# The gated-linear-attention layer rewritten as one block, with tile passes, direct context states and a four-unit scan

## The chip, the cores and the metric

One Trainium2 chip, one core of it. The metric is the device time of one launch in microseconds (us). The kernel runs on five engines that have their own instruction queues and meet only at semaphores: TensorE (PE, matrix products; PEld are its weight loads), VectorE (DVE), ScalarE (ACT), GpSimd (POOL), and SyncE (SP), which here issues DMA transfers.

## What is computed

Two blocks follow each other. The first block has two layers on 256 latent and 256 context positions of width 1024; the second block is not touched. Layer 0 mixes with a gated MLP, layer 1 with bidirectional gated linear attention (GLA); behind each mixer stands a residual with a layer norm, then PEER (top-k product-key experts), then again residual and norm. The part that matters is the mixer of layer 1:

```python
def gla_chunked(q, k, v, g, s0):            # chunks of 64 positions, 4 heads, dk=128, dv=256
    b = jnp.cumsum(g.reshape(bsz, n, GLA_CHUNK, h, dk), axis=2)
    b_end = b[:, :, -1:]
    q_in = q * jnp.exp(b); k_in = k * jnp.exp(-b); k_end = k * jnp.exp(b_end - b)
    att = jnp.where(mask, jnp.einsum('bnihd,bnjhd->bnhij', q_in, k_in), 0.0)
    o_intra = jnp.einsum('bnhij,bnjhe->bnihe', att, v)
    def step(state, inp):
        qc, kc, vc, dc = inp
        o = jnp.einsum('bihd,bhde->bihe', qc, state)
        state = dc[..., None] * state + jnp.einsum('bjhd,bjhe->bhde', kc, vc)
        return state, o
    ...

def gla_mixer(...):                         # last layer: need_ctx_out is False
    o_cf, s_f = gla_chunked(qc, kc, vc, gc[:, :, 0], s0)
    o_cb, s_b = gla_reverse(qc, kc, vc, gc[:, :, 1], s0)
    o_lf, _ = gla_chunked(ql, kl, vl, gll[:, :, 0], s_f)
    o_lb, _ = gla_reverse(ql, kl, vl, gll[:, :, 1], s_b)
    return gla_readout(o_lf + o_lb, rl, gn_g, w_out)
```

The projection `h @ w_in` gives q, k (512 columns each), v and the output gate r (1024 each) and 32 columns from which the decay logs g come (`log_sigmoid` of a second small product, over 16). In this last layer the outputs of the context positions are not needed, only the two states with which their scans end. Everything is float32.

## The kernel before

Positions stand on the 128 partitions in four tiles: tiles 0 and 1 are latent, 2 and 3 context. A large product `x @ w` is done at float32 precision from two 32-bit parts each, high and low (`split_matmul`): three matmuls for each block of 128 rows of w. The weights arrive in chunks of 256 rows by 512 columns (512 KB) in `landing`; ACT casts a chunk to its high part, DVE subtracts to get the low part, PE uses both.

The program before is a row of **stages** (`stage(k)`, line 84): a block in which each engine has its list, then a barrier of all engines and a clear of semaphores. Nothing of a later stage starts before the barrier. For layer 1 `first_layer` (line 2600) runs these, one behind the other: `residual_norm` of layer 0 on four tiles (line 486), `modulated` (459), then in `gla_mixer` (1581): `turn` (324: transposes and splits the activations), `gla_gates` (1399: the two small gate products, with `log_sigmoid`, 1437), `project` of 3072 columns for all four tiles (277, over `projection`, 184: eight landing slots, four split slots, per chunk all tiles before the next), two memsets, eight calls of `gla_tile` (1462: two directions by four tiles, two stages each), `head_norm` (420), `gate_rows` (1614), `turn`, `project` with w_out; then `residual_norm`, `modulated`, and in `peer` (1134): `turn`, `project_channels` (298), a stage for the scores, and `mix_experts` (1187). Each `gla_tile` first makes the cumulative decay logs with a matmul, exponentiates, weighs q and k; then in the second stage transposes, forms the scores `att`, and moves the state through its two chunks of 64. For context tiles only the state is moved.

In layer 0 the mixer was already written otherwise: `first_mix` (line 650) is one block in which each engine has one list written out by hand, with one semaphore for every kind of event and no barrier inside. Its functions `high`, `low_part`, `turn_job` and `take` have the same names and work as in the change.

The order everywhere is the order in which the code stands. No scheduler moves anything.

## Time and profile before

| | us |
|---|---|
| device time, median of 3 runs | 4376.91 (4375.4 to 4380.63) |
| device time of the profiled execution | 4377.48 |
| its span in the trace | 4375.7 |
| PE / DVE / ACT busy, share of the span | 80% / 62% / 30% |

The profile gives for each engine its busy time, and for each group of instructions (line, operation, operands) how long one takes and what it waited for. "PEclk" or "granted clock" is the clock of TensorE, as a share of its full 2.4 GHz: 0.5 is 1.2 GHz. The duration of one matmul is modelled and overlaps the next, so what a row of matmuls costs is read from the distance between their starts. A float32 matmul that is not split appears as two records. The rows are below, in the order in which the prediction comes to them.

### The profile page before, as it was taken

To read this page: it belongs to the slowest core of one execution; us is meant where nothing else is said; L and a number is where in the kernel's file an instruction comes from. 1 tells how busy PE (TensorE), PEld (TensorE's weight loads), DVE (VectorE), ACT (ScalarE), POOL (GpSimd) and SP (SyncE) were. 2 spreads that over 40 slices of the span, in tenths; PEclk is the share of its full clock that TensorE was granted. 3 is DMA by queue.
4 is the path that set the end of the run, shared out by engine and by line. 5 is a ranking of instruction groups with operands and counts; after the bars stand their busy time and mean duration, and the time that the engine had idled before them with its cause. 6 is when DMAs were issued, how large, how long until landed. Compare 5 with 4: busy or idle time off the path is not lost. (4 is left out here: it accounts for less than half of the span.)

```text
span 4375.7 us, 38555 instructions
## 1 busy us (share of the span) xinstructions
PE 3506.1 (80%) x13528; PEld 2238.9 (51%) x13528; DVE 2702.1 (62%) x5335; ACT 1331.8 (30%) x2307; POOL 735.9 (17%) x792
## 2 busy tenths in 40 slices
PE   8697777787777777496653777776899999999998
PEld 2386233333333332174443333332888797888896
DVE  7555766776776674432346677674766565766565
ACT  6432222222222221121011222221455454555453
POOL 0000433333333332000001333331000000000000
PEclk9898899999989998696676999998999999999999
DMA  9630999999999997030013999997655555565563
GB/s 355 222 110 33 420 422 421 421 422 421 421 421 421 421 421 288 26 115 2 1 44 137 421 422 421 421 421 290 203 169 172 184 174 173 161 178 167 173 185 126
DMA packets 282609, 1140.98 MB, mean 261 GB/s; under 512 B 26377, under 2 KB 28425, under 8 KB 184109
## 3 DMA queue, kind: packets, MB, share of 16 engines
q0 software_dynamic: 110592, 805.36, 44.3%
q1 hardware_dynamic: 170924, 331.58, 23.8%
q8 instruction: 106, 1.74, 0.2%
q10 hardware_dynamic: 900, 1.61, 0.1%
q14 instruction: 87, 0.70, 0.0%
HBM read 1137.30 MB, written 1.15 MB: 260 GB/s over the span
## 5 line engine op out<-in xcount | busy, mean ns | idle before, releaser
L133 PE MATMUL psum<-rows,diag 128*128 128x512 f32 x3072 | 1499.1, 645 | 483.2 <-ACT diag L1376 483.2
L133 PEld LDWEIGHTS psum<-rows,diag 128*128 128x128 f32 x3072 | 616.2, 206 | 1365.3 <-issue 733.2
L1339 DVE CUSTOM_DVE_ANT_0 rows<-rows,psum 128x1024 f32<-128x1024 f32 x768 | 937.5, 1221 | 586.3 <-DMA rows<-in_p_uv,place 585.8
L1227 POOL DMA_INDIRECT rows<-in_p_uv,place x768 | 723.5, 942 | 1184.3 <-PE psum L133 1138.8
L2589 DVE TENSOR_TENSOR weights_low<-landing,weights_high 128x1024 fp32r<-128x1024 f32 x400 | 488.1, 1223 | 393.5 <-ACT weights_high L2210 392.6
L2210 ACT CAST weights_high<-landing 128x1024 fp32r<-128x1024 f32 x400 | 417.7, 1047 | 571.5 <-PE psum L133 389.0
L133 PE MATMUL psum<-weights_high,hT_high 128*128 128x512 f32 x960 | 380.7, 397 | 30.5 <-DVE weights_low L264 29.2
L1376 ACT ACTIVATE diag<-ident,weight 128x128 f32<-128x128 f32 x768 | 245.3, 390 | 471.9 <-DVE weight L1315 471.9
L133 PE MATMUL psum<-weights_high,hT_low 128*128 128x512 f32 x960 | 375.5, 391 | 0.0
L133 PE MATMUL psum<-weights_low,hT_high 128*128 128x512 f32 x960 | 375.3, 391 | 0.0
L1367 ACT ACTIVATE acted<-dots 128x4 f32<-128x4 f32 x192 | 39.4, 205 | 1038.4 <-DVE dots L1339 1038.4
L1815 PE MATMUL psum<-hT_high,weights_high 128*128 128x256 f32 x1024 | 291.7, 285 | 3.4 <-DVE weights_low L2589 3.4
L1816 PE MATMUL psum<-hT_low,weights_high 128*128 128x256 f32 x1024 | 290.9, 284 | 0.0
L1817 PE MATMUL psum<-hT_high,weights_low 128*128 128x256 f32 x1024 | 290.8, 284 | 0.0
L133 PEld LDWEIGHTS psum<-weights_high,hT_high 128*128 128x128 f32 x960 | 181.4, 189 | 70.5 <-issue 32.6
L133 PEld LDWEIGHTS psum<-weights_high,hT_low 128*128 128x128 f32 x960 | 181.1, 189 | 38.6
L133 PEld LDWEIGHTS psum<-weights_low,hT_high 128*128 128x128 f32 x960 | 181.5, 189 | 36.9 <-issue 0.5
L1815 PEld LDWEIGHTS psum<-hT_high,weights_high 128*128 128x128 f32 x1024 | 197.7, 193 | 5.0 <-issue 4.9
L1816 PEld LDWEIGHTS psum<-hT_low,weights_high 128*128 128x128 f32 x1024 | 197.8, 193 | 0.1
L1817 PEld LDWEIGHTS psum<-hT_high,weights_low 128*128 128x128 f32 x1024 | 197.7, 193 | 0.0
L640 DVE TENSOR_TENSOR weights_low<-landing,weights_high 128x1024 fp32r<-128x1024 f32 x96 | 114.9, 1217 | 6.5 <-ACT weights_high L607 2.9
L607 ACT CAST weights_high<-landing 128x1024 fp32r<-128x1024 f32 x96 | 100.8, 1050 | 30.9 <-DMA landing<-in_w_mod 30.0
(363 smaller groups left out, 4165.3 us busy)
## 6 DMA issues: line engine op xcount, KB each, us to landing
landing<-in_w_in SPq DMA_DIRECT2D x192, 512.0 KB, 3.9
landing<-in_w_ff SPq DMA_DIRECT2D x128, 512.0 KB, 4.4
landing<-in_w_mod SPq DMA_DIRECT2D x96, 512.0 KB, 8.4
landing<-in_w_br SPq DMA_DIRECT2D x32, 512.0 KB, 4.0
rows<-in_p_uv,place POOLq DMA_INDIRECT x768, 26.5
landing<-in_b_w_in SPq DMA_DIRECT2D x24, 512.0 KB, 4.6
landing<-in_a_w_in SPq DMA_DIRECT2D x16, 512.0 KB, 4.8
landing<-in_p_w_q SPq DMA_DIRECT2D x16, 512.0 KB, 4.9
```

The lines of the kernel that those rows point to most:

```text
L133: return k.nc.tensor.matmul(out, lhsT, rhs, start=first, stop=last)
L607: nc.scalar.copy(weights.high[:, n % splits], landing[:, n % ring]).then_inc(chunk_high, 1)
L640: nc.vector.tensor_tensor(weights.low[:, n % splits], landing[:, n % ring], weights.high[:, n % splits].bitcast(F32), ALU.subtract).then_i ...
L1227: k.nc.gpsimd.indirect_dma_start(rows[:, n % ROW_RING, :], None, k.given["p_uv"], bass.IndirectOffsetOnAxis(place[:, g % 4, c:c + 1], 0))\
L1339: V.tensor_tensor_reduce(u, u, token, 1.0, 0.0, ALU.mult, ALU.add, dots[:, g % 4, c:c + 1]).then_inc(k.dots_done, 1)
L1367: k.nc.scalar.activation(acted[:, g % 4, 4 * q:4 * q + 4], dots[:, g % 4, 4 * q:4 * q + 4], ACT.Gelu_apprx_tanh).then_inc(k.gelu_done, 1)
L1376: k.nc.scalar.activation(diag[:, n % DIAG_RING, :], k.ident[:, :], ACT.Copy, scale=weight[:, g % 4, c:c + 1]).then_inc(k.diag_set, 1)
L1815: nc.tensor.matmul(to, mine.high, tokens.high, start=first, stop=False, skip_group_check=True)
L1816: nc.tensor.matmul(to, mine.high, tokens.low, start=False, stop=False, skip_group_check=True)
L1817: mm = nc.tensor.matmul(to, mine.low, tokens.high, start=False, stop=last, skip_group_check=True)
L2210: S.copy(weights.high[:, n % SPLITS], landing[:, n % LANDING]).then_inc(chunk_high, 1)
L2589: V.tensor_tensor(weights.low[:, n % SPLITS], landing[:, n % LANDING], weights.high[:, n % SPLITS].bitcast(F32), ALU.subtract).then_inc(ch ...
```

## The change

`first_layer` becomes `first_block`. Layer 0 keeps `first_mix` and `mix_experts`; behind them, everything from the residual norm of layer 0 to the scores of layer 1 becomes one new function, `second_mix`, one block without a barrier inside, and `mix_experts` follows as before. `residual_norm` is still used once, at the end. `gla_gates`, `gla_tile`, `gla_mixer`, `head_norm`, `modulated`, `turn`, `projection`, `peer` and others go. What `second_mix` does otherwise than the stages before:

- **Passes.** One pass is one tile (128 positions) by one group (512 columns, four chunks): 24 matmuls of 128x512. The four chunks of a group stay resident through its passes (`SPLITS = 5`, `LANDING = 3`); in the last pass of a group each chunk is set free as it is used. k and v are projected for four tiles, q and r only for the two latent ones.
- **Norms.** The residual norm of layer 0 and the modulation of layer 1 are folded: the gains and shifts are multiplied together once (`gains`), so that h comes from x in two operations; the normed x itself is made later. The same is done before PEER.
- **Gates.** One split product for both directions (`gates_low`), the bias as a 17th row of the second product, the factor 1/16 in the mask matrices, the `1 +` in the Ln's bias.
- **Context states** as direct sums (`context_sums`, `first_state`): exp of the sum of all later (or earlier) logs, times k, times v over both context tiles. No scan over the context.
- **Latent scan in four units** (`UNITS`): (direction, tile) = (0,0), (1,1), (0,1), (1,0). Between their parts stand passes 15, 16 and 17.
- **Readout.** The layer norm's 1/root goes in as a diagonal matrix in place of the identity in the transposes of y, the gain `b_gn_g` into w_out's split.

The core of the diff, with what the prediction speaks of:

```diff
+def second_mix(k, x, h, g, scores):
+    LANDING, SPLITS = 3, 5
+    GROUPS = [(w_in, NC), (w_in, 2 * NC), (w_in, 3 * NC), (w_in, 0), (w_in, 4 * NC), (w_in, 5 * NC),
+              (w_out, 0), (w_out, NC), (w_q, 0), (w_q, NC)]
+    ORDER = (2, 3, 0, 1)
+    PASSES = [(of, t) for of in range(3) for t in ORDER] + [(of, t) for of in range(3, 6) for t in (0, 1)] \
+        + [(of, t) for of in range(6, 8) for t in (1, 0)] + [(8, None), (9, None)]
+    UNITS = ((0, 0), (1, 1), (0, 1), (1, 0))
...
+        @block.sync
+            sp.dma_start(g2_rows[:, 1, :], row(0, 1, 5)).then_inc(g2_landed[1], 16)
+            for j, part in enumerate((1, 0)):
+                sp.dma_start(m_rows[:, j, 1, :], row(1, 1, part)).then_inc(m_rows_landed[1], 16)
+            for n in range(COUNT):
+                if n >= LANDING:
+                    sp.wait_ge(chunk_low, n + 1 - LANDING)
+                sp.dma_start(landing[:, n % LANDING, :, :], ...)
+                if n == 16:
+                    wait_pass(sp, 9)
...
+                if n == 18:
+                    sp.wait_ge(ctx_keys, 4)
...
+        @block.tensor
+            for j, (t, p) in enumerate(((2, None), (3, 0), (0, 1), (1, None))):
+                pe.wait_ge(h1_set, j + 1)
+                turn_tile(h, t)
+                if p is not None:
+                    pe.wait_ge(turn_low, 2 * p + 2)
+                    one_pass(p)
+            for p in (2, 3):
...
+                one_pass(p)
+            gates_low()
+            for p in range(4, 14):
+                if p == 6:
...
+                    gates_z(0)
+                if p == 8:
+                    gates_z(4)
+                if p == 11:
...
+                    context_sums()
+                if p == 12:
...
+                    decays()
+                if p == 13:
...
+                    first_state(0)
...
+                    unit_decays(0)
+                pe.wait_ge(act_taken, p - 1)
+                one_pass(p)
+            first_state(1)
+            one_pass(14)
+            for u in range(4):
...
+                    pe.wait_ge(o_set, u)
+                unit_turn(u)
+                unit_update(u, 0)
+                if u < 3:
+                    pe.wait_ge(unit_exp, u + 1)
+                    unit_decays(u + 1)
...
+                unit_att(u)
+                if u < 3:
+                    pe.wait_ge(act_taken, 15 + u)
+                    one_pass(15 + u)
+                if u < 2:
+                    unit_update(u, 1)
+                unit_out(u)
+            for t, p in ((1, 18), (0, 19)):
+                pe.wait_ge(y_set, p - 17)
+                pe.wait_ge(y_diag_set, p - 17)
+                turn_tile(y, t, y_diag)
...
+                one_pass(p)
+            for p in (20, 21):
+                pe.wait_ge(dve_taken, p - 19)
+                one_pass(p)
+            for j, t in enumerate((1, 0)):
+                pe.wait_ge(h2_set, j + 1)
+                turn_tile(h, t)
...
+            queries(8)
+            queries(9)
+            pe.wait_ge(keys_landed, 32)
+            score(0)
+            score(1)
...
-def first_layer(k, x, layer, h):
-    streams = 1 if layer == DEPTH - 1 else 2
-    if layer == 0:
...
-    else:
-        modulated(k, x, h, 2, layer, 1, 0)
-        gla_mixer(k, h)
-        residual_norm(k, x, h, streams, layer, 2, 0)
-        modulated(k, x, h, streams, layer, 4, 3)
-        peer(k, h, 2 * streams, layer)
-    residual_norm(k, x, h, streams, layer, 5, 1)
+def first_block(k, x, h):
...
+        second_mix(k, x, h, g, scores)
+        mix_experts(k, h, scores, 2, 1)
+    residual_norm(k, x, h, 1, 1, 5, 1)
```

What stood in a row before and what stands there now, at three places. First DVE, at the start of the stretch, right behind the last of layer 0's experts. Before (`rows`, `affine` are the broadcast gate and gain rows):

```order
L504 TENSOR_TENSOR h<-h,rows 128x1024 [waits loaded0]
L504 TENSOR_TENSOR h<-h,rows 128x1024 x3
L507 SCALAR_TENSOR_TENSOR x<-x,h 128x1024 [waits vector_step]
L507 SCALAR_TENSOR_TENSOR x<-x,h 128x1024 x3
L387 BN_STATS stats<-x 128x6 [waits vector_step]
L387 BN_STATS stats<-x 128x6 x7
L390 BN_AGGR moments<-stats 128x2 [waits vector_step]
L390 BN_AGGR moments<-stats 128x2 x3
```

Now (`g_rows` the gate rows, `m_rows` the modulation, `n_rows` the norm's gain and shift):

```order
L1545 TENSOR_TENSOR h<-h,g_rows 128x1024 [waits g2_landed1]
L1547 SCALAR_TENSOR_TENSOR x<-x,h 128x1024 [waits gla_step]
L1550 BN_STATS stats<-x 128x6 [waits gla_step]
L1550 BN_STATS stats<-x 128x6
L1552 BN_AGGR moments<-stats 128x2 [waits gla_step]
L1554 TENSOR_SCALAR spread<-moments 128x1 [waits gla_step]
L1558 SCALAR_TENSOR_TENSOR r<-m_rows,n_rows 128x1024 [waits gla_n_rows_landed,gla_m_rows_landed1]
L1559 SCALAR_TENSOR_TENSOR m_rows<-m_rows,n_rows 128x1024
L1561 TENSOR_TENSOR m_rows<-m_rows,r 128x1024 [waits gla_step]
L1575 SCALAR_TENSOR_TENSOR h<-x,moments,m_rows 128x1024 [waits gla_step]
L1579 RECIPROCAL inverse<-root 128x1 [waits gla_root]
L1581 SCALAR_TENSOR_TENSOR h<-h,inverse,m_rows 128x1024 [waits gla_step]
```

Before, DVE does one step for all four tiles and then the next; now it carries one tile through all steps, and the second, third and fourth tile follow in the same manner. Second, PE in the scan of a latent tile. Before (`z` holds v, `ke` the weighed k):

```order
L133 MATMUL psum<-qT,kT 128x128 [waits vector_step]
L133 MATMUL psum<-qT,kT 128x128 x7
L133 MATMUL psum<-z,ke 128x256 x4
L133 MATMUL psum<-z,att 128x256 [waits vector_step]
...
L133 MATMUL psum<-z,ke 128x256 [waits states]
L133 MATMUL psum<-z,ke 128x256 x3
L133 MATMUL psum<-state,qT 128x256 x4
L85 UNCONDITIONAL_BRANCH
L1473 UNCONDITIONAL_BRANCH [waits barrier_Pool_Activation_PE_DVE_SP_release]
```

Now, unit 0 (`h` holds v, `unit_e` the weighed q and k, `masks` the cumulative matrices):

```order
L1069 MATMUL psum<-ident,unit_e 128x128 [waits unit_keys,unit_clear,state_set]
L1069 MATMUL psum<-ident,unit_e 128x128 x7
L122 MATMUL psum<-h,unit_e 128x256 x4
L122 MATMUL psum<-g,masks 128x512 [waits unit_exp]
L122 MATMUL psum<-g,masks 128x512
L122 MATMUL psum<-qT,kT 128x64 [waits k_copied,q_copied,gla_act_taken]
L122 MATMUL psum<-qT,kT 128x64 x7
L122 MATMUL psum<-weights_high,latT_high 128x512 [waits gla_low,gla_act_taken]
...
L122 MATMUL psum<-h,unit_e 128x256 [waits stepped]
L122 MATMUL psum<-h,unit_e 128x256 x3
L122 MATMUL psum<-h,att 128x256 [waits stepped,att_set]
L122 MATMUL psum<-state,qT 128x256 x2
```

The barrier behind the tile is gone, the next unit's decay sums and a whole pass of the projection stand between the scores and the outputs, and the states of both chunks are taken in one accumulation. Third, DVE at the end, between the last pass of w_out and the queries of PEER (new rows only; before, this was `residual_norm`, `modulated` and `turn` in stages of their own):

```order
L1715 TENSOR_TENSOR h<-psum,kk 128x512 [waits gla_step,gla_used]
L1718 SCALAR_TENSOR_TENSOR x<-x,h 128x512 [waits gla_dve_taken]
L1720 BN_STATS x_stats<-x 128x6 [waits gla_step]
L1725 BN_AGGR x_moments<-x_stats 128x2 [waits gla_step]
L1727 TENSOR_SCALAR x_spread<-x_moments 128x1 [waits gla_step]
L1728 SCALAR_TENSOR_TENSOR h<-x,x_moments,late 128x1024
L1731 RECIPROCAL x_inverse<-x_root 128x1 [waits gla_root]
L1733 SCALAR_TENSOR_TENSOR h<-h,x_inverse,late 128x1024 [waits gla_step]
L1530 TENSOR_TENSOR weights_low<-landing,weights_high 128x1024 [waits gla_high]
L1536 TENSOR_TENSOR latT_low<-psum,latT_high 128x4x128 [waits gla_turn_high] x4
```

What was three stages is one chain of eight operations and the four splits of the turned tiles, and a chunk's low part stands inside it.

## Rows read from the trace of the kernel before

**Rows 1.** Start and end of the stretch, timeline: start us, us, engine, line, what.

```profile
1735.58 1.01 ACT L1357 COPY h<-psum 128x1024 f32<-128x1024 f32 x1 [7.16 <-PE psum L133]
1742.42 4.63 DVE L504 TENSOR_TENSOR h<-h,rows 128x1024 f32<-128x1024 f32 x4 [15.31 <-DMA rows<-modulation]
2375.41 0.48 DVE L1236 MAX8 s<-scores 128x8 f32<-128x128 f32 x2
```

**Rows 2.** Stages of the stretch: busy PE, PEld, DVE, ACT, POOL; granted clock, DMA share, GB/s.

```profile
1735.00:1768.00 33.00, 0.54 (x2) 0.00 (x0) 24.62 (x30) 2.50 (x3) 0.00 (x0) 0.54 0.18 64
...
1794.00:1840.00 46.00, 39.36 (x80) 10.00 (x80) 6.89 (x10) 0.00 (x0) 0.00 (x0) 0.85 0.06 16
1840.00:1862.00 22.00, 0.00 (x0) 0.00 (x0) 13.44 (x4) 9.80 (x4) 0.00 (x0) 0.50 0.00 0
1862.00:2006.00 144.00, 133.50 (x576) 109.99 (x576) 43.38 (x48) 25.26 (x24) 0.00 (x0) 0.96 0.27 88
2006.00:2248.00 242.00, 138.31 (x448) 98.02 (x448) 76.98 (x154) 18.62 (x41) 11.34 (x16) 0.66 0.00 1
2248.00:2300.00 52.00, 28.13 (x112) 23.06 (x112) 26.04 (x47) 15.20 (x17) 0.00 (x0) 0.75 0.27 92
2300.00:2325.00 25.00, 0.00 (x0) 0.00 (x0) 17.22 (x20) 0.20 (x1) 0.00 (x0) 0.52 0.31 103
2325.00:2375.00 50.00, 37.88 (x240) 35.58 (x240) 18.61 (x29) 13.39 (x20) 0.31 (x1) 0.80 0.24 86
```

**Rows 3.** Start of the projection on DVE and PE, and PE near its end, timeline.

```profile
1867.08 1.23 DVE L264 TENSOR_TENSOR weights_low<-landing,weights_high 128x1024 fp32r<-128x1024 f32 x1 [5.65 <-ACT weights_high L228]
1868.46 0.77 PE L133 MATMUL psum<-weights_high,hT_high 128*128 128x512 f32 x1 [29.23 <-DVE weights_low L264]
...
1869.45 0.63 PE L133 MATMUL psum<-weights_high,hT_low 128*128 128x512 f32 x1
1869.87 0.63 PE L133 MATMUL psum<-weights_high,hT_high 128*128 128x512 f32 x1
...
1998.39 0.39 PE L133 MATMUL psum<-weights_high,hT_high 128*128 128x512 f32 x1
1998.62 0.39 PE L133 MATMUL psum<-weights_low,hT_high 128*128 128x512 f32 x1
```

**Rows 4.** Unsplit float32 products on PE in `gla_gates`, the scan and `turn`, timeline.

```profile
1785.28 5.40 PE L340 MATMUL psum<-ident,h 128*128 128x128 f32 x32 [49.74 <-PEq L88]
...
1807.62 1.02 PE L133 MATMUL psum<-hT_high,wg 128*16 128x512 f32 x2
1808.48 1.02 PE L133 MATMUL psum<-hT_low,wg 128*16 128x512 f32 x2
...
2027.25 3.77 PE L133 MATMUL psum<-z,ke 64*128 64x256 f32 x8
...
2091.20 1.99 PE L133 MATMUL psum<-state,qT 128*128 128x256 f32 x8
```

**Rows 5.** Groups of DVE and ACT in the stretch: busy us, mean ns, idle before.

```profile
L264 DVE TENSOR_TENSOR weights_low<-landing,weights_high 128x1024 fp32r<-128x1024 f32 x32 | 38.3, 1221 | 46.3 <-ACT weights_high L228 46.1
L228 ACT CAST weights_high<-landing 128x1024 fp32r<-128x1024 f32 x32 | 33.3, 1051 | 112.1 <-PE psum L133 98.3 <-DMA landing<-in_b_w_in 12.3 <-PEq L234 1.6
L1578 DVE TENSOR_TENSOR o<-o,psum 128x512 f32<-128x512 f32 x16 | 11.0, 685 | 0.4
```

**Rows 6.** DMA issues in two parts of the stretch: KB each, median us to landing.

```profile
rows<-modulation SPq DMA_DIRECT2D x6, 512.0 KB, 5.4
landing<-in_b_w_out SPq DMA_DIRECT2D x8, 512.0 KB, 9.3
```

**Rows 7.** `first_mix` of layer 0, windows: its passes, and its queries.

```profile
310.00:320.00 10.00, 10.00 (x46) 8.28 (x45) 7.34 (x10) 1.61 (x2) 0.00 (x0) 1.00 0.00 0
360.00:370.00 10.00, 9.71 (x83) 9.47 (x81) 1.36 (x3) 1.77 (x4) 0.00 (x0) 1.00 0.01 2
```

**Rows 8.** A table load on ACT in the scan, timeline.

```profile
2019.16 1.28 ACT L1498 ACT_TABLE_LOAD   x1
```

1187 lines of the change are left out of this document (731 added, 456 removed).

## The prediction

> **What bounds the kernel now.** I first took the two ends of the stretch that the change replaces. The last expert product of layer 0 ends as ACT starts its copy at 1735.6; the experts of layer 1 begin with DVE's first MAX8 at 2375.4 [rows 1]. The stretch is 639.8 us long. Outside it the instructions are the same, so 4377.5 - 639.8 = 3737.7 us stay, measured against the profiled execution, which lies 0.6 us above the median of the three runs. The only question is how long the new stretch is.
>
> The table of stages [rows 2] shows why it can shrink. PE is busy for about 380 of those 640 us, at whatever clock it was granted. In the scan (242 us) it is busy 138 us at a granted clock of 0.66; in the norms (33 and 25 us) and in the log-sigmoid (22 us) it does nothing and DVE works alone. Only the projection (144 us, busy 133.5, clock 0.96) is filled. So no engine bounds the stretch; barriers do, each with one chain of dependent work behind it.
>
> **Prices.** At full clock split 128x512 matmuls start 0.227 us apart, and just after idle 0.43 (1869.45 to 1869.87, 1998.39 to 1998.62) [rows 3]. A pass of 24 is thus 5.44 us. An unsplit float32 product of 512 columns (two records) costs 0.86 (1807.62 to 1808.48), four of 256 columns about 1.75 to 2.0 at full clock and 3.8 at half, and a 128-column transpose 0.17 on a mean of slow and fast, 5.40 us for 32 [rows 4]; I take 0.21 cold and 0.12 warm. DVE needs 1.22 for 128x1024 and 0.69 for 128x512, ACT 1.05 for a chunk [rows 5]. A 256-column split matmul is 0.12 (83 in 9.7 us) [rows 7].
>
> **The new stretch, step by step.** I walked the four lists (PE, DVE, ACT, SP) against each other with these prices.
>
> Head, until the second pass is issued. The first row load still lands 6.8 us after the start (1735.6 to 1742.4) [rows 1]. Then DVE alone sets the pace, because PE's first pass needs low parts that stand behind norms in DVE's list. Up to `low_part(3)` that list holds three residual sums with their moments (2 x 1.22 + 2 x 0.61 + 0.4 for the small steps = 4.05 each), two gain folds (3.66 each), three norms (2.65 each), four turn jobs (0.69) and four low parts (1.22): 12.2 + 7.3 + 8.0 + 2.8 + 4.9 = 35.2 us. To this come waits. Eleven transfers of 512 KB are now asked for at once on two queues, where the old stage asked for four; at the 5.4 us that a row takes to land behind its neighbours [rows 6], the norm rows come about 1.5 us and the chunks that ACT's first root stands behind about 3 us after DVE wants them: 4.6. The last quarter of pass 0 at half clock (2.6) and the turn of tile 0 (1.7) follow: 4.3. Head = 6.8 + 35.2 + 4.6 + 4.3 = 50.9. Those waits could be nothing (-4.6), or each load could take as long as the slowest chunk landing, 9.3 us [rows 6] (+5); I stay near the 5.4, since these are the same kind of load.
>
> Middle, on PE, from pass 1 to pass 14. Here PE is the longest engine. Thirteen of the fourteen passes 1 to 14 at 5.44 each = 70.7, pass 1 itself 5.44 + 2.4 for twelve cold matmuls (12 x 0.2) = 7.8; a turn 1.2; `gates_low` 48 matmuls of at most 256 columns at 0.12 = 5.7 (it replaces 32 unsplit products at 0.86, 27.5 us); the eight gate products 6.9; six context sums 5.2; `decays` 3.8 (16 products of two columns, bounded by their weight loads at 0.24); two `first_state` 6.9; the first unit's sums 1.7. Sum 109.9. DVE has about 45 us of work in this time and ACT about 55, six table loads among it, so both hide. What they could cost is a wait at `gates_z` or `context_sums`: there the logs must be ready two passes later, and by my walk they are ready 2 and 6 us early. Of the q and r projections of context tiles six passes are gone, 32.6 us at full clock.
>
> Units, u = 0 to 3. Each has the transposes (1.0), an update (1.7), the next unit's sums (1.7), scores (1.7), a pass (5.4), a second update (1.7), outputs, 12 products of 256 columns (5.2), and ACT's or DVE's two copies before the next unit may overwrite the banks (1.4): 19.8, twice. Unit 2 has no second update, but DVE's copies for ACT's: 18.3. Unit 3 has neither pass nor sums to cover its copies and masks (2.6): 13.8. Sum 71.7. The eight old scan tiles took 242 [rows 2].
>
> Tail, to the first MAX8. Turn and split of y tile 1 (3.2), pass 18 (5.4), wait for the second readout and its diagonals (1.0), turn and split of tile 0 (3.0), passes 19 to 21 (16.3); then almost nothing on PE while DVE does three low parts (3.7), takes the last result (2.1), ends the norm of tile 0 (2.9), does one more low part (1.2) and four splits (2.8): 12.7; queries, 8 chunks of 24 x 0.12, and 2.4 cold = 25.4; scores and the last copy 7.7; barrier 1.3. Sum 76.0.
>
> Together 50.9 + 109.9 + 71.7 + 76.0 = 308.5. Not in it are about 35 hand-overs between engines at 0.15 us, as between a low part's end (1867.08 + 1.23) and PE's start (1868.46) [rows 3], and two more cold starts of 2.4 in the tail: I add 10. The bounds of this term are 0 and, if each hand-over cost 0.7 us as one small DVE operation does [rows 5], 25. The new stretch is 319 us, and **the forecast is 3737.7 + 319 = 4057 us**.
>
> **A rule weighed.** A table load on ACT takes 1.28 us here [rows 8], and the new list has eight in the stretch (sqrt, exp and ln twice, exp, silu, sqrt). I count them at that price, beside PE's passes. The Trainium skill ("ScalarE: Activation LUTs", What ACT_TABLE_LOAD costs) says that a switch also pays a drain, together about 2.66 us. By that page, and if all eight were on the path, the estimate would be 4068; the trace shows only the 1.28.
>
> **Rivals.**
>
> A, the clock stays low in the units. In the scan before, PE had a granted clock of 0.66 though it was busy more than half of the time [rows 2], and the first matmuls after a wait go at half speed [rows 3]. Unsplit products then cost double (3.8 against 2.0) [rows 4]. Against it: in the units the waits are 1 to 2 us and dense passes stand between, and `first_mix`, written in the same way, has 1.00 throughout its passes [rows 7]. About 64 us of the units are PE work; at 0.66 they cost 33 more, at half 64: 4090, at the far end 4121. The Trainium skill ("TensorE: Matmul & The Clock Gate", HAM oscillation) describes this for kernels whose bursts are shorter than their waits; by that rule units without passes would stay cold, and here only unit 3 is one.
>
> B, a list waits in the wrong order. Each engine's list is fixed, and one late event (ACT's logs before `context_sums`, a chunk of w_out behind `late` in SP's queue, DVE's chain before the queries) holds all behind it. Nothing in the profile before shows such a list for this layer; PE's idle rests in `first_mix`'s passes are nil [rows 7]. If the waits sum to 30 us instead of 10 the time is 4077, if to 45, 4092.
>
> C, fewer waits than I allow: the 10 us don't appear and the head's 4.6 neither: 4043.
>
> D, slower than before. The ring is shorter: three landing slots instead of eight, and every chunk's transfer is asked for only when the low part of three chunks earlier is done. If the transfers did not overlap at all, a chunk would cost landing 9.3 + cast 1.05 + low part 1.22 = 11.6 us, 40 chunks 463, and with the head's 51 and a tail of 30 the time would be 4282. It becomes slower than before only if a chunk costs over 14 us; at 16 it would be 3737.7 + 640 + 81 = 4459. Nothing in the rows comes near.
>
> E, the change doesn't do what it says: PE's list shows passes between the parts of the units, so only the waits are open.
>
> **Chances.** Forecast 55% (its own range 4045 to 4073), A 12%, B 19%, C 12%, D 1%, something else 1%. The range from 4032 to 4098 takes in C, B and A's nearer end and the bounds of head and hand-overs. Faster by over 0.2% (8.8 us, about what a measurement of this kernel can tell from no change) 98%, within it 1%, slower 1%.
>
> **What will show it.** In the changed profile: DVE's first sum about 6.8 us after the experts' last product, pass 1 on PE about 51 us after it; granted clock 1.0 and starts 0.227 apart from pass 2 on; pass 14 ending near 161 us; units about 20, 20, 18 and 14 us long; an idle PE of about 10 us before the queries and the first MAX8 about 319 us after the start. Wrong would be: a clock below 0.9 in the units (A), a wait of over 3 us in front of a pass (B), or `mix_experts` and what follows changed by more than 5 us, which would break the first subtraction.

## The result and the profile after

The changed kernel takes **4050.61 us** (median of four runs, 4047.85 to 4052.42), the kernel before 4376.15 (four runs beside it, 4375.07 to 4380.63): a ratio of 0.925, 95% interval 0.9239 to 0.9262, so 325.5 us less. The forecast was 4057, with a range from 4032 to 4098. The profiled execution took 4050.69 us, its span is 4048.9, and the mean granted clock over it is 0.936.

The ends of the stretch in the changed kernel, in the timeline (start us, us, engine, line, operation); they answer to [rows 1]:

```profile
1736.40 1.01 ACT L2001 COPY h<-psum 128x1024 f32<-128x1024 f32 x1 [7.16 <-PE psum L122]
...
1742.87 1.23 DVE L1545 TENSOR_TENSOR h<-h,g_rows 128x1024 f32<-128x1024 f32 x1 [14.95 <-DMA g_rows<-modulation]
...
2050.76 0.48 DVE L1880 MAX8 s<-scores 128x8 f32<-128x128 f32 x2
```

The stretch is 2050.76 - 1736.40 = 314.4 us long instead of 639.8. Outside it are 4050.69 - 314.4 = 3736.3 us, against 3737.7 before: the experts did not change, and all of the gain lies in the stretch.

What stood there before as stages [rows 2] is now one block. The windows over it (length, then busy time and count of PE, PEld, DVE, ACT, POOL; granted clock, DMA share, GB/s): the whole stretch, then head, middle, units and tail as the prediction cut them, then the four units.

```profile
1736.40:2050.76 314.36, 250.47 (x1228) 204.33 (x1228) 169.32 (x253) 114.84 (x178) 3.23 (x6) 0.90 0.29 91
1736.40:1792.40 56.00, 13.70 (x49) 10.87 (x49) 38.07 (x47) 10.56 (x15) 1.24 (x3) 0.61 0.47 153
1792.40:1900.80 108.40, 106.70 (x490) 84.52 (x489) 45.49 (x52) 53.58 (x79) 1.85 (x2) 0.98 0.34 108
1900.80:1975.30 74.50, 68.41 (x325) 53.82 (x324) 41.81 (x87) 27.57 (x47) 0.00 (x0) 0.98 0.19 57
1975.30:2050.80 75.50, 61.66 (x368) 55.13 (x368) 43.99 (x68) 23.18 (x38) 0.14 (x1) 0.91 0.18 56
1900.80:1921.40 20.60, 19.46 (x93) 15.08 (x91) 11.14 (x20) 8.87 (x14) 0.00 (x0) 1.00 0.34 103
1921.40:1942.10 20.70, 19.51 (x93) 15.16 (x93) 10.23 (x20) 3.88 (x8) 0.00 (x0) 1.00 0.00 1
1942.10:1960.80 18.70, 17.36 (x84) 13.78 (x84) 12.40 (x24) 8.12 (x14) 0.00 (x0) 1.00 0.29 86
1960.80:1975.30 14.50, 12.08 (x56) 9.80 (x57) 8.04 (x25) 6.70 (x11) 0.00 (x0) 0.88 0.09 35
```

The same query over the old stretch, as one window of the kernel before:

```profile
1735.58:2375.41 639.83, 382.58 (x1488) 281.83 (x1488) 241.68 (x358) 89.55 (x119) 11.79 (x18) 0.74 0.14 46
```

Put side by side, the two whole-stretch rows split the gain in two. PE's busy time fell from 382.6 to 250.5 (132 us: less work, and the same work at 0.90 of the clock instead of 0.74). Its idle time fell from 257 to 64 us (193 us). DVE's busy time fell too, from 242 to 169, while ACT's rose from 90 to 115: ACT took over work, beside PE.

| part | forecast | measured |
|---|---|---|
| outside the stretch | 3737.7 | 3736.3 |
| head, to pass 1 | 50.9 | 56.0 |
| middle, pass 1 to unit 0 | 109.9 | 108.4 |
| units | 71.7 (19.8, 19.8, 18.3, 13.8) | 74.5 (20.6, 20.7, 18.7, 14.5) |
| tail | 76.0 | 75.5 |
| hand-overs, not placed | 10 | none is left over |

So three things were to be explained: the head is 5.1 us too long, the units 2.8, and the 10 us for hand-overs did not appear. The head first. ACT in its first 26 us (ACTq is its DMA queue):

```profile
1741.32 0.60 ACTq L1279 DMA_DIRECT2D wg<-in_b_w_in  x1
1741.95 7.72 ACTq L1282 DMA_DIRECT2D w<-in_b_w_gate  x1
...
1750.49 3.83 ACTq L1282 DMA_DIRECT2D w<-in_b_w_gate  x1
...
1758.46 0.45 ACTq L1289 DMA_DIRECT2D gain<-in_b_gn_cols  x1
1758.96 1.99 ACT L1309 CAST weights_high<-landing 128x1024 fp32r<-128x1024 f32 x2 [21.55 <-issue]
1760.96 1.28 ACT L1320 ACT_TABLE_LOAD   x1
1762.26 0.20 ACT L1320 ACTIVATE root<-spread 128x1 f32<-128x1 f32 x1
```

And DVE, which needs that root:

```profile
1749.67 1.23 DVE L1558 SCALAR_TENSOR_TENSOR r<-m_rows,n_rows 128x1024 f32<-128x1024 f32 x1 [2.57 <-DMA n_rows<-in_ln_b]
...
1762.49 0.16 DVE L1579 RECIPROCAL inverse<-root 128x1 f32<-128x1 f32 x1 [7.88 <-ACT root L1320]
```

DVE had the variance ready at 1747.1 and waited for the root from 1754.6 on; the root, 0.2 us of work, came at 1762.3. Ahead of it in ACT's list stood the issue of its loads (until 1758.9, with two issues that took 7.72 and 3.83 us), the casts of the first two chunks, and a table load. DVE's waits in the head are 2.57 + 7.88 = 10.45 us where the prediction had 4.6. In the DMA issues of this window a chunk of w_in took 14.8 us to land and the norm's rows 8.7 and 10.7, where [rows 6] had 9.3 for a chunk and 5.4 for a row:

```profile
landing<-in_b_w_in SPq DMA_DIRECT2D x3, 512.0 KB, 14.8
...
n_rows<-in_ln_g ACTq DMA_DIRECT2D x1, 512.0 KB, 8.7
n_rows<-in_ln_b ACTq DMA_DIRECT2D x1, 512.0 KB, 10.7
```

Two theories for the head stood against each other. **Issue**: ACT's sequencer is blocked by its own 20 loads. **Data and order**: eleven and more transfers of 512 KB share the DMA engines, and the root stands in the wrong place of ACT's list.

### The profile page after: what moved, and what is told of

The parts are those of the page before. It is cut to its first block and busy times, and to the rows that moved or that the text cites. A ratio compares the mean times of both kernels' runs of the same rounds, so it can differ in the third digit from the quotient of the medians.

```text
span 4048.9 us, 37069 instructions
## 1 busy us (share of the span) xinstructions
PE 3380.2 (83%) x13268; PEld 2162.0 (53%) x13268; DVE 2630.6 (65%) x5231; ACT 1357.4 (34%) x2366; POOL 729.1 (18%) x780
## 5 line engine op out<-in xcount | busy, mean ns | idle before, releaser
L122 PE MATMUL psum<-weights_high,hT_high 128*128 128x512 f32 x768 | 304.7, 397 | 1.3 <-DVE hT_low L2649 1.3
L122 PE MATMUL psum<-weights_high,hT_low 128*128 128x512 f32 x768 | 299.8, 390 | 0.0
L122 PE MATMUL psum<-weights_low,hT_high 128*128 128x512 f32 x768 | 299.8, 390 | 0.0
L122 PEld LDWEIGHTS psum<-weights_high,hT_high 128*128 128x128 f32 x768 | 144.7, 188 | 32.2 <-issue 1.8
L122 PEld LDWEIGHTS psum<-weights_high,hT_low 128*128 128x128 f32 x768 | 144.6, 188 | 30.9
L122 PEld LDWEIGHTS psum<-weights_low,hT_high 128*128 128x128 f32 x768 | 144.8, 189 | 29.1 <-issue 0.5
L315 ACT CAST weights_high<-landing 128x1024 fp32r<-128x1024 f32 x96 | 100.8, 1050 | 30.9 <-DMA landing<-in_w_mod 30.0
```

The lines of the kernel that those rows point to most:

```text
L122: return k.nc.tensor.matmul(out, lhsT, rhs, start=first, stop=last)
L315: nc.scalar.copy(weights.high[:, n % splits], landing[:, n % ring]).then_inc(chunk_high, 1)
```

## Experiments on the head

**Small loads away from ACT.** The gate weights, masks and small vectors (15 loads) are issued by POOL, which has little to do there.

```diff
+            # in POOL's list, behind its first three memsets
+            pool.wait_ge(wg_clear, 1)
+            for j in range(2):
+                pool.dma_start(wg[...], w_in[...]).then_inc(wg_landed, 16)
...
-            act.wait_ge(wg_clear, 1)
-            for j in range(2):
-                act.dma_start(wg[...], w_in[...]).then_inc(wg_landed, 16)
...
```

> The changed kernel with one edit: the 15 small loads of second_mix (gate weights, masks, member, gain) are issued by POOL instead of ACT. In the changed kernel ACT spends 1738.0 to 1758.9 issuing them, 7.7 and 3.8 us of it on the two loads that stand behind the gathers of the gate columns, and DVE waits 7.9 us for the first root. Theory 1 (ACT's list is the cause, the issue blocks behind the gathers): chunk 0 has landed long before, the root comes 6 to 9 us earlier, DVE's wait falls to under 2 us, head 56 to 48..50 us, time 4050.6 to 4042..4045. Theory 2 (the data are the cause: eleven big loads share the DMA engines, and chunk 0 lands late anyway): the wait stays over 5 us and the time within 3 us of 4050.6.

Measured: 4046.83 us (4043.14 to 4052.09), ratio to before 0.925 (0.9235 to 0.9266); stretch 310.0 against 314.4. DVE's reciprocal stood 24.2 us after the start instead of 26.1. ACT, in this run's timeline:

```profile
1754.62 1.05 ACT L1310 CAST weights_high<-landing 128x1024 fp32r<-128x1024 f32 x1 [19.08 <-DMA landing<-in_b_w_in]
1756.11 1.05 ACT L1310 CAST weights_high<-landing 128x1024 fp32r<-128x1024 f32 x1 [0.44 <-DMA landing<-in_b_w_in]
1757.17 1.28 ACT L1321 ACT_TABLE_LOAD   x1
1758.46 0.20 ACT L1321 ACTIVATE root<-spread 128x1 f32<-128x1 f32 x1
```

ACT's queue was now free and ACT still waited, for the chunk: "<-issue" has become "<-DMA landing". That alone would say that the issue cost almost nothing. But the chunk did not land when it did before. The first chunk's load in the changed kernel, and in this run:

```profile
landing<-in_b_w_in SPq DMA_DIRECT2D x1, 512.0 KB, 13.8
```

```profile
landing<-in_b_w_in SPq DMA_DIRECT2D x1, 512.0 KB, 16.7
```

In the changed kernel it was issued at 1739.3 and had landed at 1753.1, 16.7 us after the start, and ACT came to it at 1758.96: its own issues held it for 5.8 us. In this run it landed 20.1 us after the start, and DVE's wait for the rows grew from 2.57 to 4.34 us. The small loads were now all issued 11.5 us after the start instead of 22.5, beside the large ones; whether that, or the other queue, made the large ones land later was not taken apart. So both theories hold a part: the issue was removed (DVE's wait for the root fell from 7.88 to 4.29), later landings took most of it back, and the head gained 2 us. The result lies between the two expectations. Of the 4.4 us by which the stretch is shorter, 1.7 are a higher clock in unit 3 (below). The medians are only 3.8 us apart, about as much as the runs of one kernel scatter, so these sizes rest on the traces.

**The root first.** On top of that, the norm's two row loads stand first in ACT's queue, and the first root ahead of the casts.

```diff
-            act.dma_start(g2_rows[:, 0, :], row(0, 0, 5)).then_inc(g2_landed[0], 16)
             for j, name in enumerate(("ln_g", "ln_b")):
                 act.dma_start(n_rows[:, j, :], ...)
+            act.dma_start(g2_rows[:, 0, :], row(0, 0, 5)).then_inc(g2_landed[0], 16)
...
+            first_root(0)
             high(0)
             high(1)
-            first_root(0)
```

> small_on_pool with two more moves: the norm's second row load stands first on ACT's queue, and ACT's first root stands ahead of its casts of chunks 0 and 1 in ACT's list. Theory ACT's order: DVE's first reciprocal stood 24.2 us after the start in small_on_pool, of which 4.3 us were a wait for a root that was queued behind two casts and a table load; with the root ahead of them the reciprocal comes 3 to 5 us earlier and the stretch is 305 to 307 us long against 310.0, time 4042 to 4044. Rival, the landing itself: the rows and chunks share the DMA engines, and what DVE gains it waits again for the first low part, because chunk 0 lands no earlier and is now cast later: the reciprocal is earlier but pass 0 and pass 1 stay where they were, 35 us and about 54 us after the start, and the time stays 4047.

Measured: 4044.51 us (4040.97 to 4046.39), ratio 0.9237 (0.9221 to 0.9252); stretch 307.6. ACT:

```profile
1746.34 0.20 ACT L1321 ACTIVATE root<-spread 128x1 f32<-128x1 f32 x1 [4.60 <-DVE spread L1555]
1755.66 1.04 ACT L1310 CAST weights_high<-landing 128x1024 fp32r<-128x1024 f32 x1 [9.12 <-DMA landing<-in_b_w_in]
```

The root now comes at once, and DVE's reciprocal 19.7 us after the start, 4.5 earlier than in the run before, within what the theory of ACT's order expected (3 to 5). Of the 4.5, 4.3 are the wait for the root. Moving the norm's rows forward brought only 0.2: DVE still waits 4.11 us at the same place, now for the modulation rows (`m_rows`); pass 0 begins 30.8 us after the start instead of 35.3 and pass 1 49.6 instead of 54.1, so the rival (nothing moves on, because the chunk lands no earlier) is refuted. The chunk did land no earlier (20 us after the start in both), but DVE has other work until then. The stretch shortened by 2.3 only: at the first unit 3.6 us of the 4.5 were left, and unit 3 gave back 1.6 (its clock, below). The time and the stretch lie about 0.5 us above the ranges that were expected.

## Experiments on the tail

PE's longest wait after the units is for the second normed tile. In the changed kernel DVE stood as follows before it, and PE behind it:

```profile
2003.96 3.49 DVE L1530 TENSOR_TENSOR weights_low<-landing,weights_high 128x1024 fp32r<-128x1024 f32 x3
2007.37 0.68 DVE L1715 TENSOR_TENSOR h<-psum,kk 128x512 f32<-128x512 f32 x1
```

```profile
2012.58 1.12 PE L992 MATMUL psum<-ident,h 128*128 128x128 f32 x4 [7.39 <-DVE h L1733]
```

Three low parts that only the queries need stand before the result that everything waits for.

**Tail reordered.** They go behind the last norm, and the turn of the first tile ahead of it. ACT's list is put in the same order (its part of the edit is left out here).

```diff
             last_norm(0)
-            for n in range(33, 36):
-                low_part(n)
+            for j in range(12, 14):
+                turn_job(j, latT, 1 - (j - 12) // 2)
             take(21)
             last_norm(1)
-            low_part(36)
-            for j in range(12, 16):
+            for j in range(14, 16):
                 turn_job(j, latT, 1 - (j - 12) // 2)
-            for n in range(37, 40):
+            for n in range(33, 40):
                 low_part(n)
```

> The changed kernel with one edit: in the tail, DVE's low parts of chunks 33 to 35 and 36 move behind the last norm and the last turn jobs (ACT's cast of chunk 36 likewise), since PE can't use them before the queries start. They stand 3.5 + 1.2 us in DVE's chain from the end of pass 21 to the queries. Theory 1 (that chain is the path): PE's start of the queries moves 4 to 5 us earlier against pass 21's end, time 4050.6 to 4046 +- 1. Theory 2 (the queries then wait for their second chunk's low part, as they wait for the first now): gain under 2 us.

Measured: 4048.21 us (4045.51 to 4049.22), ratio 0.9247 (0.9232 to 0.9263); tail 73.1 instead of 75.4. Only half of what was expected. DVE's list shows why:

```profile
2003.75 1.29 DVE L1538 TENSOR_TENSOR latT_low<-psum,latT_high 128x512 fp32r<-128x512 f32 x2 [1.37 <-ACT latT_high L1314]
2004.96 0.68 DVE L1717 TENSOR_TENSOR h<-psum,kk 128x512 f32<-128x512 f32 x1
```

The turn jobs that took the low parts' place cost 1.29 and, being at the end of a chain over PE and ACT, a wait of 1.37 in front of them: of the 3.4 us of low parts only 0.8 were gained (PE's wait is 6.63 instead of 7.39), and the rest of the 2.3 came behind it. One late event at the head of a list again held what stood behind it.

**Both early moves** (small loads on POOL, the tail, and in the head low part 3 ahead of DVE's second gain fold and third norm):

> The changed kernel with the edits of small_on_pool and tail_order together, and low_part(3) in DVE's head before the second gain fold instead of behind the third norm, so that pass 0 does not wait for it. If the two waits are independent the gains add: -8, -4.5, and -2 from the head's order, time 4036 +- 3. If ACT's and DVE's lists only move the wait elsewhere, 4041 or more.

Measured: 4043.51 us (4039.05 to 4048.11), ratio 0.9242 (0.9227 to 0.9257), stretch 306.9. That is the second of the two expectations: the gains did not add up to 4036. The first unit begins 4.3 us earlier than in the changed kernel and the tail is 1.5 shorter; the other 1.7 are the clock of unit 3.

**All moves, and all turn jobs behind `last_norm(1)` on DVE** (against the run before; the two moves of the run with the root first are not shown again).

```diff
             last_norm(0)
-            for j in range(12, 14):
-                turn_job(j, latT, 1 - (j - 12) // 2)
             take(21)
             last_norm(1)
-            for j in range(14, 16):
+            for j in range(12, 16):
                 turn_job(j, latT, 1 - (j - 12) // 2)
             for n in range(33, 40):
                 low_part(n)
```

> root_first, and low_part(3) ahead of one of DVE's turn jobs, and in the tail the last norm and the turn of tile 0 ahead of low parts 33 to 39. Theory: PE's wait for the second turn of the tail (7.4 us in the changed kernel, of which 3.5 us were low parts ahead of it in DVE's list) goes, the low parts fall beside passes 18 to 21, and the tail is 4 to 5 us shorter than 75.4; together with the head the stretch is 301 to 304 us and the time 4036 to 4041. Rival: the low parts are then late for passes 19 to 21 and PE waits for them instead; the tail stays at 73 to 75 and the time is 4042 to 4045, as the run with both earlier moves.

Measured: **4038.44 us** (4037.17 to 4039.20), ratio to before 0.9226 (0.921 to 0.9241); stretch 303.3, tail 71.5. It is the fastest of all: its slowest run is 8.6 us below the fastest of the changed kernel. PE's wait for the second turn:

```profile
2002.05 1.97 PE L1006 MATMUL psum<-ident,h 128*128 128x128 f32 x8 [4.35 <-DVE h L1736]
```

From 7.39 to 4.35, as the theory expected, and the rival (PE waits for low parts instead) is refuted. So of the changed kernel's 314.4 us, 11 were the order of a few instructions: 6.9 before the first unit, 4.0 in the tail. Unit 3 has the lower clock in both kernels, so the clock has no part in this difference.

## Experiments on the units

**Passes ahead of the units.** The three passes that stand inside units 0 to 2 run before them, with their casts and copies on ACT and their low parts on DVE.

```diff
             one_pass(14)
+            for u in range(3):
+                pe.wait_ge(act_taken, 15 + u)
+                one_pass(15 + u)
             for u in range(4):
...
                 unit_att(u)
-                if u < 3:
-                    pe.wait_ge(act_taken, 15 + u)
-                    one_pass(15 + u)
```

> The changed kernel with one edit: passes 15, 16 and 17 stand in front of the four scan units instead of inside units 0 to 2 (casts, low parts and takes of their chunks moved with them). Theory 1 (the passes in the units cover the waits for copies, masks and state, some 2.5 us per unit, and nothing else): three units lose that cover, +7 to +9 us, granted clock stays at 1.0 in the units, 4058. Theory 2, rival A of the prediction (without dense passes PE's clock falls in the units as in the old scan, 0.66): units of about 20 us each instead of 15, +20 to +35 us, 4071 to 4086. Theory 3 (nothing to cover): within 3 us.

Measured: 4057.11 us (4053.84 to 4059.78), ratio 0.9272 (0.9256 to 0.9287); 6.5 us slower by the medians, 3.0 in the trace. The window of its four units:

```profile
1916.87:1975.79 58.92, 50.58 (x254) 39.44 (x252) 34.14 (x79) 17.40 (x34) 0.00 (x0) 1.00 0.11 36
```

The prediction's rival A was that the clock would be low in the units. Here they have no dense passes between their parts, PE is idle 14% of the time, and the clock is 1.00 throughout. What the passes covered is read from units 0 to 2, which ran at 1.00 in both kernels: they take 46.1 us here (1916.87 to 1962.99), and in the changed kernel 60.0, of which three passes are 16.3, so 43.7. The three passes covered 2.4 us inside the units. Another 2.4 stand ahead of the units, where the passes now follow each other and each waits for ACT to clear its banks, three times like this:

```profile
1898.48 0.49 PE L122 MATMUL psum<-weights_high,latT_high 128*128 128x512 f32 x1 [0.68 <-ACT r L1337]
```

So interleaving is worth 4.8 us in the trace, 1.6 a pass. The trace's stretch is only 3.0 us longer, because unit 3 ran at full clock here and gave 1.7 back. The medians say 6.5, and the profiled execution is the fastest of this run's four; what is left between 3.0 and 6.5 is open. The first theory (cover lost, clock kept) came out, a little below its 7 to 9 us.

The prediction took from the Trainium skill ("TensorE: Matmul & The Clock Gate", HAM oscillation) that units without passes would stay cold. The Trainium skill describes there bursts of work that are shorter than the waits between them. Here the waits are 1.0 to 1.4 us and the work between them is several times as long, so the units without passes are another case, and this run doesn't test it. The low clock of the old scan (0.66, [rows 2]) went with longer idle rests, such as the 5.05 us in a row of the next section; here PE's longest wait is 1.4.

Unit 3 alone is a small case of the rival. It has a granted clock of 0.88 and takes 14.5 us in the changed kernel; in the run with the small loads on POOL the same instructions ran at 1.00:

```profile
1956.04:1968.84 12.80, 10.39 (x56) 8.64 (x57) 8.04 (x25) 6.71 (x11) 0.00 (x0) 1.00 0.10 38
```

That is 1.7 us, in one unit. The kernels with both early moves, with the passes ahead and with doubled passes also have 12.8 us there; those with the root first, with the tail reordered and with all moves have 14.3 to 14.5. PE's wait in front of it is 1.38 us in all of them; which of their differences decides it stays open. With two landing slots (below) it is worse.

## Parts of the change alone, in the kernel before

**Direct context states only.** The four context tiles of the scan are replaced by one load of masks and one stage, everything else as before.

```diff
-            for direction, tiles in ((0, (2, 3, 0, 1)), (1, (3, 2, 1, 0))):
+            context_states(k, z, g, state)
+            for direction, tiles in ((0, (0, 1)), (1, (1, 0))):
...
+                matmul(k, k.psum[:, 0, :], after[:, :], g_of(0, 2), True, False)
+                matmul(k, k.psum[:, 0, :], every[:, :], g_of(0, 3), False, True)
...
+                            mm = matmul(k, k.psum[...], ce[:, 2 * d + t, a * P:(a + 1) * P],
+                                        z[:, 2 + t, D + a * DV:D + (a + 1) * DV], t == 0, t == 1)
```

> The kernel before with one part of the change alone: the context states as direct sums. Four of the eight scan tiles (about 24.2 us each) are gone; in their place stand one load of three 128x128 masks and one stage of six 256-column products, four exponentials, four multiplications, sixteen 256-column products and four copies, about 25 to 30 us with its load. Theory: the barriers and chains of the scan tiles are a large part of what the change gains, and this part alone brings 97 - 27 = 70 us: 4306, between 4300 and 4316. Rival: most of the gain is the overlap of passes with everything else, and the direct sums bring less because their unsplit products run at a low clock and the stage is one chain: the new stage costs 45 us or more, the time is 4325 or above.

Measured: 4298.89 us (4296.16 to 4304.10), ratio 0.9824 (0.9807 to 0.984): **77.6 us** less. PE in the new stage, up to the first remaining tile:

```profile
2016.54 2.05 PE L133 MATMUL psum<-g,after 128*128 128x512 f32 x2 [15.63 <-PEq L88]
...
2024.67 7.07 PE L133 MATMUL psum<-z,ce 128*128 128x256 f32 x32
2033.49 1.10 PE L133 MATMUL psum<-g,prefix 128*128 128x512 f32 x2 [1.75 <-PEq L88]
...
2075.84 0.45 PE L1516 MATMUL psum<-ident,qi 128*128 128x128 f32 x1 [5.05 <-PEq L88]
```

From its first product to that of the next tile the stage takes 17 us, and its load puts 3.5 us in front (15.63 of idle time where the kernel before has 12.13); together they stand for four tiles of about 24. The estimate of 27 for both was high, and the time lies 1 us below the expected range (4300 to 4316), on the side of the theory. The last row is PE's first product of a latent tile's second stage, behind an idle rest of 5.05 us, in which the chain through ACT and DVE runs.

**Split gate product only.**

```diff
+        split(k, wg[:, :, :], wgs.part(slice(None), slice(None), slice(None)))
...
-                        for part in (hT.high, hT.low):
-                            mm = matmul(k, k.psum[0:GLA_RANK, j, :], wg[...], part[:, b, :].bitcast(F32), ...)
+                        mm = split_matmul(k, k.psum[0:GLA_RANK, j, :], wgs.part(...), hT.part(slice(None), b), ...)
```

> The kernel before with one part of the change alone: the low-rank gate product as split products. 32 unsplit products of 0.86 us (27.5 us) become 48 split ones at 0.227 (10.9 us), and a split of the 128x512 gate weights is added (about 2 to 3 us, with its barrier). Theory, price of unsplit products: 14 us faster, 4362. Rival, the clock: the products stand in a stage that begins cold, so both forms run partly at half clock, and 48 cold ones of 0.43 cost 20.6: 4 us faster only, 4372.

Measured: 4362.77 us (4360.01 to 4365.18), ratio 0.9968 (0.9957 to 0.998): **13.7 us** less. The first product of this run, and the one behind the last:

```profile
1800.92 0.58 PE L133 MATMUL psum<-hT_high,wgs_high 128*16 128x512 f32 x1 [9.91 <-PEq L88]
...
1815.30 1.12 PE L133 MATMUL psum<-w,low 16*128 16x512 f32 x2 [0.77 <-DVE low L1428]
```

The 48 products took 13.6 us rather than 10.9, since the first go at 0.43 (1801.31, 1801.73, 1802.16), but the old ones start cold too and took 29.3 (1799.09 to 1828.38): the difference came out as computed.

**Ten empty stages** ahead of the scan:

```diff
+            for _ in range(10):
+                with stage(k):
+                    pass
             for direction, tiles in ((0, (2, 3, 0, 1)), (1, (3, 2, 1, 0))):
```

> The kernel before with ten stages that hold no work, put between the log-sigmoid and the eight scan tiles. It prices one barrier. Theory, barriers are cheap by themselves and cost by the chains they end: 1.1 to 1.5 us each, as the barrier behind the stretch's last copy, so 11 to 15 us, time 4388 to 4391. Rival, each barrier costs more (instruction lists of five engines, a first wait): 2.5 us or more each, 25 us in all, 4402; then the stages of the old stretch would have cost a large part of the 326 us that the change gained.

Measured: 4383.57 us (4382.05 to 4387.35), ratio 1.0011 (1.0002 to 1.0021), which is 1 to 9 us for ten. PE's first product of the scan in the kernel before, and in this run:

```profile
2014.08 2.05 PE L133 MATMUL psum<-g,prefix 128*128 128x512 f32 x2 [12.13 <-PEq L88]
```

```profile
2024.64 2.05 PE L133 MATMUL psum<-g,prefix 128*128 128x512 f32 x2 [19.56 <-PEq L88]
```

PE is idle 7.43 us longer: **0.74 us for a barrier** whose stage is empty, below both expectations. (The whole stretch is 10.6 us longer in this trace; 3.9 of that stand before PE's rest, where the two kernels are the same, and show how much one trace differs from another.) The barriers themselves were a small part of what was gained. What they cost in the old stretch is what stood idle on both sides of them, such as the 5.05 us above.

## Is the middle bound by PE, and is three landing slots enough?

**Six passes run twice** (4, 5, 6, 8, 9, 10, over the same operands, so nothing else changes):

```diff
-                for pair in range(4):
+                for pair in range(4) if p not in (4, 5, 6, 8, 9, 10) else (0, 1, 2, 3, 0, 1, 2, 3):
```

> The changed kernel with passes 4, 5, 6, 8, 9 and 10 computed twice over the same operands (the same sums are started again, so the output is unchanged): the PE work of six passes more, 144 products, as many as the change leaves out for the context's queries and readout gates. Theory, PE sets the middle and those six passes were worth their full 32.6 us: middle 141, time 4083. Rival, the middle is in part set by what DVE and ACT prepare (high and low parts every 2.3 us of DVE's time, 45 us in all): then the extra products fill waits and the time rises by less than 27 us, under 4078.

Measured: 4080.78 us (4078.48 to 4085.27), ratio 0.9322 (0.9305 to 0.9339): **30.2 us** more by the medians. The window from pass 1 to the first unit:

```profile
1791.30:1930.60 139.30, 139.30 (x635) 111.89 (x634) 45.68 (x52) 54.44 (x79) 1.85 (x2) 0.98 0.26 84
```

139.3 against 108.4 in the changed kernel: 30.9 of the 32.6 us that 144 products at 0.227 cost. The rest filled a wait of 1.7 us for ACT that PE has there. So PE bounds the middle, and the six passes that the change leaves out were worth 30 us (31 in the middle; unit 3 gave 1.7 back at full clock).

**Two landing slots instead of three.**

```diff
-    LANDING, SPLITS = 3, 5
+    LANDING, SPLITS = 2, 5
```

> The changed kernel with two landing slots instead of three for the 40 chunks of weights; it is the point from which the rival of a too short ring decides. Theory, slack: a chunk takes some 6 to 9 us to land behind its request and PE uses two per 5.4 us, so with two slots a pass of two chunks can't be faster than about one landing and one cast and low part (9 to 11 us): the middle's 14 passes grow from 5.4 to 8 or more and the time rises by 30 to 60 us: 4080 to 4110. Rival, the transfers are short when few are queued (512 KB at the 370 GB/s measured in the head is 1.4 us): time rises by under 8 us.

Measured: 4065.40 us (4064.07 to 4067.82), ratio 0.9286 (0.9269 to 0.9303): 14.8 us more, below the one expectation and above the other. The stretch grew by 16.9: 3.7 before the units, 6.3 in them, 6.9 in the tail. Of the 6.3 most is one unit's clock. PE now waits 3.34 us in front of unit 3 (1.38 in the changed kernel), and the unit itself takes 18.8 us for 14.5:

```profile
1965.08:1983.90 18.82, 16.41 (x56) 13.17 (x57) 8.04 (x25) 6.70 (x11) 0.00 (x0) 0.64 0.08 27
```

The other 2.0 are that longer wait. So rival A is real in kind: 2 us more of waiting, and unit 3 ran at 0.64 with the same instructions. Whether the longer wait alone did it was not tested. ACT's wait for the chunks of the queries' weights in the tail (what, total, times, longest), in the changed kernel and in this run:

```profile
ACT weights_high L1309 <- DMA landing<-in_p_w_q: 2.3, 1, 2.3
```

```profile
ACT weights_high L1309 <- DMA landing<-in_p_w_q: 6.0, 2, 5.2
```

PE's wait for the second normed tile grew with it, since DVE's low parts and norms stand in one list:

```profile
PE psum L992 <- DVE h L1733: 12.1, 2, 11.0
```

My expectation took every pass to use new chunks. In the passes up to the units it doesn't hold: a group of four chunks serves four passes, later two, so the next group has 22 or 11 us to land, and two slots do almost as well as three. In the units and the tail a late chunk delays a list in which ACT and DVE have other duties, and PE waits for these. With three slots ACT's one wait of this kind in the tail is 2.3 us.

## Why the prediction came out 6 us high

The parts that were summed give 308.5, 5.9 less than the 314.4 measured; with the 10 for hand-overs the forecast was 4.1 more. Outside the stretch the time is 1.4 less than was taken over. So two errors of opposite sign (head and units too short, a term for waits that did not come) stood behind a result that is 6 us off, and a part of that nearness is luck.

**Where it was right.** The cut of the time into what stays and a stretch (3737.7 against 3736.3) and the statement that barriers and their chains bound the old stretch: 193 of the 325 us are PE's idle time. The middle (109.9 against 108.4) was summed from product counts and the distances of [rows 3, 4 and 7], and the doubled passes show that this was the right kind of sum, since PE is busy in 106.7 of those 108.4 us. Two small terms in it offset each other: pass 1 was priced with 2.4 us of cold products and ran at full clock from its third product on, and a wait of 1.7 us for ACT was not in the sum. The gate product was priced by [rows 4] at 27.5 against 5.7 for its new form; alone in the old kernel a split form saved 13.7 where the same prices gave 14. The tail came out at 75.5 for 76.0, with its idle rest before the queries at 11.7 us (2005.19, where PE runs dry, to 2016.84, where the queries start, with the second tile's turn in it) for 12.7. The table loads are 1.28 us here too, eight in the block, and the next activation starts 1.29 or 1.30 after each load's start:

```profile
1829.74 1.28 ACT L1349 ACT_TABLE_LOAD   x1
1831.03 2.19 ACT L1349 ACTIVATE x<-x 128x512 f32<-128x512 f32 x4
1833.24 1.28 ACT L1353 ACT_TABLE_LOAD   x1
```

The drain that the Trainium skill adds ("ScalarE: Activation LUTs", What ACT_TABLE_LOAD costs) can't be seen in these rows, and the estimate of 4068 worked out from that page's figure was further off than the sum from rows.

**Step that was mis-sized: the head's waits (4.6, measured 10.45).** "The norm rows come about 1.5 us and the chunks that ACT's first root stands behind about 3 us after DVE wants them." The mechanism is there, with both of its releasers in the trace (2.57 for the rows, 7.88 for the root). The price of 5.4 us for a landing, taken from a stage with four transfers at once, was wrong for a dozen: the rows took 8.7 and 10.7, a chunk 14.8. The upper bound that the text gave (5 us more, by the 9.3 of the slowest chunk landing) happened to be nearly what was measured, but for another reason. The first chunk had landed at 1753.1, before DVE asked for the root. What held the root until 1762.3 was the issue of 20 loads on ACT's queue, until 1758.9, and behind it two casts and a table load (1.99 + 1.28). The prediction counts the eleven large transfers and not what their and the 15 small loads' issue costs ACT; it had seen that the root stands behind the chunks and had not asked what the casts and the table load add there. The run with the small loads on POOL shows that removing the issue alone brings 2 us, since the large loads then land later; the root's place in ACT's list was worth 4.3 us more. The rest of the head was right: 56.0 - 6.5 - 10.45 = 39.1 for the list and the start of PE, summed as 35.2 + 4.3 = 39.5.

**Step that was wrong: the 10 us of hand-overs.** The prediction added 35 hand-overs at 0.15 and two cold starts, beside sums that had been made from distances between starts and from walks that already ended in waits. Measured against the parts, nothing is left for them: middle -1.5, tail -0.5, and what the head and the units took beyond their sums has other causes. A hand-over counts only where PE waits, and in the middle it does once. In the units, where waits do end parts, they were priced (1.4, measured 1.16 twice):

```profile
1921.42 1.09 PE L1069 MATMUL psum<-ident,unit_e 128*128 128x128 f32 x8 [1.16 <-ACT x L1396]
1942.08 1.09 PE L1069 MATMUL psum<-ident,unit_e 128*128 128x128 f32 x8 [1.16 <-ACT x L1396]
```

So the units' +2.8 is not waits. In units 0 to 2 (+2.1) it is PE's work: 19.5 busy where 18.4 was summed. In unit 3 (+0.7) it is the clock, which cost 1.7; at full clock it takes 12.8, 1.0 less than forecast. An update costs 1.9 (1912.89 to 1914.81), as [rows 4] had at full clock, while the sum took 1.7; the outputs took 5.5 for 5.2.

**The rivals.** A (low clock): it did not come, by the windows above and by the units without passes; only unit 3 has a little of it (1.7 us), and the run with two slots shows that it was not far away (0.64 in unit 3). B (a list in the wrong order): true in kind at two places, the root in the head and the low parts in the tail, and small in size; undoing both brought 11 us, not the 20 to 35 that B named as extra waits. C (fewer waits, 4043) named the 10 us rightly and the head wrongly. D (the ring): one slot fewer costs 15 us (4.3 of them by unit 3's clock), so the ring has little to spare, but it was far from what D needed. Its point of decision, 14 us a chunk, was reached once, by the first three chunks (14.8), and did not matter there, since only the rate over 40 chunks would. E did not happen.

**Where the 325 us came from.** Three parts were measured each alone: the direct context states 78 and the split gate product 14 in the kernel before, the six passes 30 in the changed one. They add to 122. About 204 us are left for the fusion: norms, logs and the latent scan beside passes, and no chain between barriers. That share is a difference, not a measurement of its own, and it takes for granted that the three parts are worth the same in either kernel. The empty stages show that only a small part of it is the price of barriers: at 0.74 us, even fifty would be 37.

## What to carry to other kernels

When several stages become one block, sum the engine that stays busy by distances between starts, and add nothing for hand-overs where it has a queue of work (here the middle came out 1.5 us under such a sum); put the care into the two ends, where one engine's list is the path. There, write down for each list what stands ahead of the first small result that another engine waits for (DMA issues, casts, a table load), and price loads by how many are asked for at once rather than by a quiet stage's landing time. A barrier is cheap; the chain that it ends is not: the direct sums replaced eight stages by two and brought 78 us, of which six barriers at 0.74 are 4. And when a single trace differs by 2 us, look at the granted clock of each part first: unit 3 alone moved by 1.7 between kernels that did not touch it.

## What the runs showed of the hardware that I had not expected

- Issuing one DMA on ACT's queue can block ACT for long: the gate weights' issues took 7.72 and 3.83 us where the other issues took 0.3 to 1.0, each directly behind the issue of one of the two loads of `wg` (64 KB in short rows of 16 numbers), while the DMA engines were full. In the run that moved these loads to POOL the same issues took 0.56 and 0.50 us there, and ACT was free; whether the short rows or the full engines make the block was not taken apart.
- A 512 KB load took 5.4 us to land in a stage with four such loads and 13.8 to 15.8 with a dozen in flight; with 15 small loads issued earlier beside them it was 16.7 to 18.1.
- A barrier of all five engines with the clear of its semaphores costs 0.74 us by PE's idle time over ten of them; the 95% interval of the times gives 0.1 to 0.9.
- PE kept its full clock (1.00) in 59 us of units with 14% of idle time in waits of at most 1.4 us, and lost part of it (0.88) in some kernels in the last unit, whose instructions are the same. Behind a wait of 3.34 us instead of 1.38 that unit had 0.64.
